# Experts ranked by their tokens on the chip: four of eight work on 64 slots instead of 96

## What is computed

```python
def swiglu(h, w1, w3, w2):
    return (jax.nn.silu(h @ w1) * (h @ w3)) @ w2

def moe_swiglu(h, w_r, b_r, w1, w3, w2):
    logits = (hf @ w_r).astype(jnp.float32) + b_r.astype(jnp.float32)
    top_v, top_i = lax.top_k(logits, TOP_K)          # 2 of 8
    gates = jax.nn.softmax(top_v, axis=-1)
    combine = jnp.sum(jax.nn.one_hot(top_i, N_EXPERTS) * gates[..., None], axis=-2)
    for e in range(N_EXPERTS):
        out = out + combine[:, e:e + 1] * swiglu(hf, w1[e], w3[e], w2[e])
```

## Time and profile before

| | |
|---|---|
| median of three runs | 1546.9 us (1544.61 to 1548.57) |
| the profiled execution | 1545.36 us, of which the span from the first to the last instruction is 1543.2 us |
| PE busy | 1482.5 us, 96% of the span |
| weight loads of PE | 856.9 us, 56% |
| DVE / ACT busy | 544.0 us (35%) / 409.7 us (27%) |
| moved by DMA | 396.39 MB, of which 388.84 MB by the queue of SP |

### The profile page before, as it was taken

The page is one execution under the profiler, slowest core; times in us unless marked ns, Lnnn a source line. Parts: engine busy times, 40 slices in busy tenths (PEclk is TensorE's granted clock), DMA queues, the critical chain, the costliest instruction groups (busy, mean ns, idle before and its releaser), DMA issues.

```text
span 1543.2 us, 27247 instructions
## 1 busy us (share of the span) xinstructions
PE 1482.5 (96%) x12261; PEld 856.9 (56%) x12261; DVE 544.0 (35%) x967; ACT 409.7 (27%) x719; POOL 4.1 (0%) x8
## 2 busy tenths in 40 slices
PE   6899889999999999898889999999999999999997
PEld 3688558888888888787673333333333333333332
DVE  2899884432323333779741110020111002011112
ACT  3522684422222222665830011010001101000001
POOL 0000000000000000000000000000000000000010
PEclk9999899999999999999989999999999999999999
DMA  9988702623321433313167999999999999999991
GB/s 352 385 302 321 281 29 82 208 67 109 109 82 39 152 105 114 110 55 148 44 246 261 396 407 342 408 355 411 403 402 407 343 408 366 410 398 382 408 382 43
DMA packets 147323, 396.39 MB, mean 257 GB/s; under 512 B 7584, under 2 KB 38848, under 8 KB 147200
## 3 DMA queue, kind: packets, MB, share of 16 engines
q1 hardware_dynamic: 144000, 388.84, 66.8%
q10 hardware_dynamic: 2624, 3.63, 0.7%
q0 software_dynamic: 576, 2.10, 0.4%
HBM read 390.74 MB, written 3.80 MB: 256 GB/s over the span
## 4 chain that ended last, share of the span: by engine, by line
PE 88%; DVE 6%; DMA 3%; ACT 1%; SPq 1%; issue 1%; DVEq 0%; ACTq 0%
PE bank L1107 30%; PE bank L1137 10%; PE bank L953 5%; PE bank L954 5%; PE bank L952 5%; PE bank L1145 5%; PE bank L675 4%; PE bank L676 3%; PE bank L677 3%; DMA weight_ring<-in_w_ada 3%; PE bank L961 3%; PE bank L962 2%; PE bank L963 2%; PE bank L621 2%; DVE weight_ring L1793 1%; DVE slot_halves L1700 1%
## 5 line engine op out<-in xcount | busy, mean ns | idle before, releaser
L1107 PE MATMUL bank<-weight_ring,gathered 128*32 128x512 f32 (+1 forms) x4608 | 464.1, 557 | 0.0
L1107 PEld LDWEIGHTS bank<-weight_ring,gathered 128*32 128x32 f32 x4608 | 146.5, 110 | 291.9 <-issue 290.7
L1137 PE MATMUL bank<-weight_ring,scratch 128*32 128x512 f32 x1360 | 165.9, 592 | 0.0
L2138 DVE TENSOR_TENSOR scratch<-scratch,bank 64x512 f32<-64x512 f32 (+1 forms) x72 | 46.0, 639 | 316.9 <-ACT scratch L1608 314.0
L954 PE MATMUL bank<-slot_halves,slot_halves 128*128 128x512 f32 x336 | 130.7, 389 | 0.0
L953 PE MATMUL bank<-hT_halves,slot_halves 128*128 128x512 f32 x336 | 130.7, 389 | 0.0
L952 PE MATMUL bank<-slot_halves 128*128 128x512 f32 x320 | 124.6, 389 | 0.0
L1793 DVE SCALAR_TENSOR_TENSOR weight_ring<-scratch,conv_weights,weight_ring 128x512 f32<-128x512 f32 (+1 forms) x207 | 121.3, 636 | 2.6 <-ACT weight_ring L1385 0.7
L676 PE MATMUL bank<-hT_halves,slot_halves 128*128 128x512 f32 (+1 forms) x352 | 121.6, 346 | 0.0
L675 PE MATMUL bank<-slot_halves,slot_halves 128*128 128x512 f32 (+1 forms) x284 | 105.4, 371 | 8.1 <-DVE slot_halves L1700 5.2
L1608 ACT ACTIVATE scratch<-bank 64x512 f32<-64x512 f32 (+1 forms) x72 | 40.1, 557 | 230.1 <-PE bank L1107 229.2
(11 more groups left out here) (298 smaller groups left out, 1681.1 us busy)
## 6 DMA issues: line engine op xcount, KB each, us to landing
weight_ring<-in_exp_w SPq DMA_DIRECT2D x216, 1024.0 KB, 10.0
weight_ring<-in_w_ada SPq DMA_DIRECT2D x24, 2048.0 KB, 13.6
weight_ring<-in_exp_w SPq DMA_DIRECT2D x64, 768.0 KB, 8.1
weight_ring<-in_ffn_w SPq DMA_DIRECT2D x33, 1024.0 KB, 5.4
weight_ring<-in_w_in SPq DMA_DIRECT2D x8, 1024.0 KB, 15.4
weight_ring<-in_w_out SPq DMA_DIRECT2D x4, 2048.0 KB, 11.4
weight_ring<-in_w_in SPq DMA_DIRECT2D x2, 3072.0 KB, 15.2
expert_rows<-scratch ACTq DMA_DIRECT2D x14, 128.0 KB, 6.0
```

Of the source, the lines that this page charges most:

```text
L1107: i = mm(ps[BLOCK * job:BLOCK * (job + 1), 0:cw], gathered_block(e, k, b), w[:, kk, a * cw:(a + 1) * cw], start=(k == 0), stop=(k == KT - 1))
L1137: i = mm(bank[6][quarter, :], at01[:, c0:c0 + BLOCK], w2[:, i_, half * 512:(half + 1) * 512], start=(first and i_ == 0), stop=(last and i_ ...
```

## The change

- Position 0 stays expert 0. On the positions 1 to 7 stand the experts 1 to 7 in an order that DVE works out in `ranked`: by their number of tokens, the four with the fewest on the positions 1, 3, 5 and 7 (`SMALL`), the three with the most on 2, 4 and 6.
- The positions in `SMALL` have two blocks (64 slots), the others three. For the small ones `pair` and `gated` do two blocks, L1090, L1145 and the copy for block 2 fall away, and so do the rows of block 2 in `rows_shifted`, `rows_scaled`, `rows_kept_of` and `scatter` (position 7 is a small one).
- Three rounds are run if any position holds more tokens than its slots.
- SP reads the expert of each position from 1 to 7 from a table in SBUF (`value_load`, after a wait on `most_ready`) and forms the address of each weight load from that register.
- The gathers are one expert ahead of the stage (96 columns instead of 192), three from g = 1 on and four from g = 7 on; `select(1)` stands ahead of the groups. PE waits ahead of `residual_rows` for the counts and no longer for `most_ready`.
- `rows_found` works with slots and first rows by position; 32 columns are added to the constants.

```diff
+SMALL = [1, 3, 5, 7]
+LARGE = [i for i in range(NE) if i not in SMALL]
+RANK_OF_POSITION = [0] + [1 + (SMALL + LARGE[1:]).index(i) for i in range(1, NE)]
+BLOCKS_OF = [2 if i in SMALL else BLOCKS for i in range(NE)]
+BLOCK_ORDER = [[1, 0] if i in SMALL else [0, 1, 2] for i in range(NE)]
 SELECTS = 4
-PLACE = [3, 4, 5, 6, 7, 1, 2, 0]
-GATHERS = [(0, 1), (2, 3, 4), (7, 5, 6)]
+PLACE = [3, 4, 5, 6, 1, 2, 3, 0]
+GATHERS = [(0,), (1, 2, 3), (7, 4, 5, 6)]
...
             def expert_weights(r):
+                expert = {}
+
+                def of_expert(name, e):
+                    return t[name][0, e] if e == 0 else t[name][0, bass.ds(expert[e], 1)].rearrange("a k n -> (a k) n")
+
                 def first(g):
                     e, j = divmod(g, CH)
                     w = WIDTH[j]
+                    if e and j == 0:
+                        sp.wait_ge(most_ready, 1)
+                        expert[e] = sp.value_load(expert_at[0:1, e:e + 1], min_val=0, max_val=NE - 1)
                     for p in range(KT // 2):
                         for m, name in enumerate(["exp_w3", "exp_w1"]):
                             v = UNITS * r + H_UNIT[g, p, m]
-                            load(v, unit(v, w), t[name][0, e].rearrange("(k p) n -> p k n", p=P)[
+                            load(v, unit(v, w), of_expert(name, e).rearrange("(k p) n -> p k n", p=P)[
                                 :, 2 * p:2 * p + 2, j * 1024:j * 1024 + w])
...
-                            i = mm(ps[:, c * 2 * C:(c + 1) * 2 * C], rows_, sel_first[n],
+                            i = mm(ps[:, c * C:(c + 1) * C], rows_, sel_first[n],
...
             def scatter(n):
 
-                for v, rows_ in ((0, rows_01), (1, rows_2)):
-                    for half in range(2):
-                        part = slice(HD * half, HD * half + HD)
-                        i = mm(bank[SCATTER_BANK[2 * n + half]][:, :], to_token[part, n, v, :], rows_[part, :],
-                               start=(v == 0), stop=(v == 1))
-                        if v == 1:
-                            i.then_inc(scatter_mm, 1)
+                for half in range(2):
+                    part = slice(HD * half, HD * half + HD)
+                    mm(bank[SCATTER_BANK[2 * n + half]][:, :], to_token[part, n, :], rows_01[part, :],
+                       start=True, stop=True).then_inc(scatter_mm, 1)
 
             def experts(r):
...
-                    pe.wait_ge(a_tok, 3 * (NG * r + g) + 3)
-                    for q in range(nq):
-                        i = pe.transpose(s2[:, q * HD:(q + 1) * HD], act_2[:, q * P:(q + 1) * P], ident[0:HD, 0:HD])
-                    i.then_inc(a_mm, 1)
+                    if g // CH not in SMALL:
+                        pe.wait_ge(a_tok, before_group(g, r, 2, 3) + 3)
+                        for q in range(nq):
+                            i = pe.transpose(s2[:, q * HD:(q + 1) * HD], act_2[:, q * P:(q + 1) * P], ident[0:HD, 0:HD])
...
                     for kk in range(2):
                         k = 2 * p + kk
-                        for b in range(BLOCKS):
+                        for b in BLOCK_ORDER[e]:
                             ps = sums(g, b)
+                            last = b == BLOCK_ORDER[e][-1]
                             for job in range(4):
                                 w = w1 if (job < 2) == (b == 1) else w3
                                 a = job % 2
                                 i = mm(ps[BLOCK * job:BLOCK * (job + 1), 0:cw], gathered_block(e, k, b),
                                        w[:, kk, a * cw:(a + 1) * cw], start=(k == 0), stop=(k == KT - 1))
-                                if kk == 1 and b == BLOCKS - 1 and a == 1:
+                                if kk == 1 and last and a == 1:
                                     i.then_inc(unit_done, 1)
-                            if k == KT - 1 and b < BLOCKS - 1:
+                            if k == KT - 1 and not last:
...
-                        if i_ == 0:
+                        if i_ == 0 and e not in SMALL:
...
-                            pe.wait_ge(most_ready, 1)
+                            pe.wait_ge(pos_ready, 2)
...
+            def ranked():
+
+                dve.wait_ge(pos_ready, 2)
+                square = parts[:, 0:NE * NE].rearrange("p (i e) -> p i e", e=NE)
+                link(stt(out=key, in0=held_by, scalar=float(NE), in1=con[:, KEY:KEY + NE], op0=ALU.mult, op1=ALU.add))
+                link(tt(square, across(key, NE), down(key), ALU.is_lt))
+                link(dve.reduce_sum(rank, square, AX))
+                link(tt(of_position, across(rank, NE), down(con[:, RANK:RANK + NE]), ALU.is_equal))
+                for n in range(2):
+                    link(tt(square, of_position, across(pv[:, :, n], NE), ALU.mult))
+                    link(dve.reduce_sum(placed[:, :, n], square, AX))
+                link(by_position(at_position, con[:, IOTA:IOTA + NE]))
+                dve.tensor_copy(expert_at[:, :], at_position)
+                link(by_position(over, held_by))
+                link(tt(over, over, con[:, CAP:CAP + NE], ALU.subtract))
+                link(dve.reduce_max(den[:, 0:1], over, AX))
+                ts(most[:, :], den[:, 0:1], float(C), None, ALU.add).then_inc(most_ready, 1)
...
-                if e == NE - 1:
-                    tt(rows_2, bank[7][:, :], gate_b, ALU.mult).then_inc(yt_ready, 1)
-                else:
+                if e not in SMALL:
                     for half in range(2):
...
+                    counted()
                     gates()
-                    fullest()
+                    ranked()
                     rows_copied()
+                select(1)
+                if r == 0:
+                    places_of_experts()
                 for g in range(NG):
                     e, j = divmod(g, CH)
                     if e and j == 1:
                         rows_scaled(e - 1, r)
-                    if g:
+                    if g and (g - 1) // CH not in SMALL:
                         second_turned(g - 1)
```

More of the change, by code:

```diff
@@ L91, with slots, first_row, before @@
 H_UNIT, Y_UNIT, UNITS = unit_numbers()
+def slots(i):
+    return BLOCK * BLOCKS_OF[i]
+def first_row(i):
+    return sum(slots(p) for p in range(i))
+def before(i, r, small, large):
+    each = [small if p in SMALL else large for p in range(NE)]
+    return r * sum(each) + sum(each[:i])
+def before_group(g, r, small, large):
+    return before(g // CH, r, CH * small, CH * large) + (g % CH) * (small if g // CH in SMALL else large)
 CONSTS = ["ident", "mean_d", "mean_head", "mean_conv", "rot", "halves", "before", "ones"]
@@ L98 @@
 REV = IOTA + ROUNDS * C
-NCONST = REV + NE
+KEY = REV + NE
+RANK = KEY + NE
+CAP = RANK + NE
+LINE = CAP + NE
+NCONST = LINE + NE
 def backbone(nc, t, out):
@@ L472, in fills_at, with fill_sums, kept_before @@
             e, j = divmod(g, CH)
[L473 to L476, removed]
+            return [(e // 2 + 1, 4 * (j - 1) + spot)] if e in (0, 2) and j else []
+        def fill_sums(g, spot):
+            return sums(g - 1, 2 - spot % 2)
         FIRST_FILL_BANK = [7, 6, 5, 3]
         SCATTER_BANK = [0, 1, 2, 5]
+        def kept_before(i, r):
+            each = [32 if p in SMALL else 64 for p in range(NE - 1)]
+            return r * sum(each) + sum(each[:i])
         pv = posm[:, 0:2 * NE].rearrange("p (e n) -> p e n", n=2)
         cv = comb[:, 0:2 * NE].rearrange("p (e n) -> p e n", n=2)
+        placed, gate_last = (att[:, a:a + n].rearrange("p (e n) -> p e n", n=2) for a, n in ((16, 2 * NE), (32, 2)))
+        of_position = scr[:, 7424:7488].rearrange("p (i e) -> p i e", e=NE)
+        parts = scr[:, 7488:7616]
+        key, rank, held_by, at_position, over, slots_by, line_by = (att[:, 40 + i * NE:48 + i * NE] for i in range(7))
         def rounds(eng, body, end):
@@ L541, in second @@
                         f0 = j * 1024 + u * 256
-                        load(v, unit(v, D), t["exp_w2"][0, e][f0:f0 + 256, :].rearrange("(q p) n -> p q n", p=P))
+                        load(v, unit(v, D), of_expert("exp_w2", e)[f0:f0 + 256, :].rearrange("(q p) n -> p q n", p=P))
                 for g in range(NG):
@@ L1149, in experts @@
                 if r:
[L1150 removed]
+                    pe.wait_ge(yt_ready, before(0, r, 1, 2))
                     pe.wait_ge(scatter_added, 4 * r)
@@ L1574, in rows_kept_of @@
             def rows_kept_of(e, r):
-                done = 2 * (NE * r + e)
                 if r:
                     act.wait_ge(row_back, 64 * r)
-                for z, (rows_, b, n) in enumerate([(rows_01, 0, HD), (rows_2, 2, BLOCK)]):
-                    act.wait_ge(yt_ready, done + z + 1)
+                for z, (rows_, b, n) in enumerate([(rows_01, 0, HD), (rows_2, 2, BLOCK)][:BLOCKS_OF[e] - 1]):
+                    act.wait_ge(yt_ready, before(e, r, 1, 2) + z + 1)
                     for half in range(2):
```

(23 more changed lines are left out.)

164 lines of the change are left out of this document (91 added, 73 removed).

## The result

The changed kernel takes 1504.5 us (median of four runs, 1504.3 to 1506.0), the kernel before 1547.4 us in the same session: ratio 0.9728, 95% interval 0.9711 to 0.9744. It is faster by 2.7%, and 18 us slower than the 1486 us forecast. The profiled execution's span is 1504.1 us, against the 1486.0 us of the sum.

What follows compares the result with a forecast made beforehand. PE set the pace with DMA close behind; after the change DMA would bound: stream from 858.5 us, plus 613.2, 2.7 and 11.6 us, a span of 1486.0 us. Forecast 1486 us, range 1468 to 1506 us.

Steps and rivals of the forecast that it cites:

- The mechanism: Expert stage: the bound moves from PE to DMA, the ring runs empty and bytes set the end, 613 us.
- A: Expert stage: PE stays the bound and its whole saving counts, 1424 us; chance 0.02.
- C: SP's weight loads: a register address makes each issue longer than 2.7 us, about 1560 us at 3 us; chance 0.03.
- D: Small positions: an expert there exceeds 64 tokens, so three rounds run, about 2850 us; chance 0.02.
- E: Expert stage: 391 GB/s is DMA's own mean, so almost nothing changes, 1544 us; chance 0.04.
- B: Small positions: PE's waits lower its clock, up to 1652 us if all run at 1.2 GHz; chance 0.04.
- Landing times: Weight loads in the expert stage: time from issue to landing grows to 30 us and more.
- PE's busy time: Whole kernel: PE's busy time falls by about 118 us.
- The head: Start of the stage: `gather_first` gains 1.5 us (bounds 0 to 3.4); later gathers lie where PE waits anyway.
- The rate: Saturated stretch: DMA moves 251.4 MB at 410 GB/s; a rate of 415 to 400 means -7 to +15 us.
- The end of the stream: Last weight loads: the stream ends at 1471.7 us; only a low clock was allowed for, 0 to +5 us.
- The tail: After the stream: 2.7 us for semaphore and last product, then 11.6 us (13.3 less 1.7) to the span's end.

Runs made afterwards that it cites:

- all_small: The changed kernel with all seven positions 1 to 7 at two blocks and the overflow check off: 1504.2 us, ratio 0.973.
- half_bytes: The changed kernel with each weight load of the four small positions bringing only half of its unit, PE's work unchanged: 1431.6 us, ratio 0.926.
- const_addr: The changed kernel with the expert addresses of positions 1 to 7 written as constants in place of the register: 1505.4 us, ratio 0.9739.
- in_flight_5: The changed kernel with SP issuing a weight load only once the load five places back has landed: 1505.0 us, ratio 0.9733.
- thin_fills: The changed kernel with the eight gathers in position 0 doing one matmul of four: 1503.6 us, ratio 0.9729.
- rows_later: The changed kernel with residual rows and gate rows moved from position 0 into position 1, same result: 1502.6 us, ratio 0.9714.

## Why the prediction was right, and where it was off

**The mechanism was right.** DMA's bytes set the end (all_small, half_bytes), PE's own time would have been some 1430 us, and the ring runs empty. PE's idle time by DMA is 41.9 us ahead of the pairs and 12.2 ahead of the products with w2, near the 60 us named; nearly all of it lies in positions 3, 5 and 7, the first 1.9 us between 980 and 1000 us in position 2. SP's waits for PE fall from 478.6 to 106.2 us between 900 and 1478 us. Of the rivals, A is the time without the bytes; C is refuted by const_addr; D did not come, one round was run; E is refuted by 407 GB/s over 578 us. The clock of B did fall, to 0.91 and 0.83 in single windows of 20 us, but over 900 to 1478 us it was 0.99, though the waits ahead of the pairs (27 of them, 1.6 us in the mean, 4.3 at the longest) were longer than the 0.8 to 1.7 us that the prediction counted on; and all_small, with 0.95 there and more waiting, is no slower.

**Two signs did not come.** Landing times were to grow to 30 us and more; they are 18.1 us in the median and 24.2 at the most, because SP stands in its issue once about seven loads are under way and doesn't queue the whole ring. And PE's busy time was to fall by 118 us; it fell by 98. In half_bytes, with the same work and no waits, it falls by 113.5, so 15 us of the gap are the slower matmuls of a PE that waits (567 ns for 559 in the pairs). With DMA as the bound neither cost anything.

**A sum of a rival was wrong.** In C, 3 us an issue would be 0.28 us too much in each of 248 units on top of an unchanged 1547 us: about 1616 us and not 1560.

**The sum was 18.1 us short**, in four terms. The median, 1504.5 us, is inside the range by 1.5 us, and there was some luck in that: the head and the end of the stream left the bounds that the prediction gave them (+1.5 and +5 us), and the rate used only 4 of its 15.

*The head: 7.4 us.* The prediction took 1.5 us of gain from `gather_first` and put the gathers for positions 1 to 3 where "PE waits anyway". In 800 to 900 us DMA moved 28.2 MB, against 30.6 MB before, where 0.6 MB more was expected: 3.0 MB at 407 GB/s are 7.4 us. (These two profiles can be compared so: their stages start within 0.06 us of each other.) One part is `gather_first` itself (now L1086). Its chain at the start of the stage in in_flight_5, which has the same code there, beside the earlier trace rows:

```profile
801.41 7.03 PE bank L1088 x32
808.44 11.87 PE bank L1162 x96
```

Half the columns take 7.03 us for 32 matmuls, no less than before (6.71): from start to start 0.21 us with 96 columns as with 192, at a granted clock of 0.50. So the lower bound of the estimate (nothing saved) was the right end. And the 96 records behind it take 11.87 us in place of 10.44: in the kernel before the clock is at 1.00 from 808 us on, in the changed kernel from 812. Why it rises later is not shown. The changed kernel itself has 7.03 and 11.85 us and is done with these records 1.8 us later than the kernel before; with the 1.5 us of gain that did not come, that is 3.3 of the 7.4 us. The other part, 4.1 us, are eight gathers (L1097) that lie in position 0 now, from 840.6 us on, ahead of saturation, when the first later gather of the kernel before starts at 897.58 us. They take PE eight times 0.72 us, 5.8 us, and there each us of PE delays the freeing of places. Here PE did not "wait anyway". thin_fills and rows_later agree: from the stage's start the last load lands 2.3 to 2.6 us sooner than in the changed kernel's two profiles for 3.1 us of PE's work, and 3.1 to 3.4 sooner for 3.4; both lie outside the scatter of the four kernels with the changed head (685.1 to 686.9), by 0.8 and 1.6 us.

*The rate: 4.2 us.* 407 GB/s were measured for the 410 taken, over 578 us. It is within the range of 405 to 415 and just under the 408 to 413 named as a sign.

*The end of the stream: 5.3 us.* In its last 11 us DMA moves 212 GB/s, 2.3 MB that at 407 take 5.7 us. The prediction let the stream stop at full rate, as it does in the kernel before. Its last windows at full rate and behind it, and then two of the changed kernel:

```profile
1500.00:1502.00 2.00, 2.00 (x31) 0.80 (x27) 2.00 (x3) 0.00 (x0) 0.00 (x0) 1.00 1.01 403
1502.00:1504.00 2.00, 2.00 (x32) 0.84 (x28) 2.00 (x2) 0.00 (x0) 0.00 (x0) 1.00 0.45 174
...
1480.00:1482.00 2.00, 1.91 (x16) 0.41 (x16) 0.00 (x0) 1.09 (x1) 0.00 (x0) 1.00 0.69 260
1484.00:1486.00 2.00, 1.06 (x16) 0.25 (x12) 0.00 (x0) 0.00 (x0) 0.00 (x0) 1.00 0.49 201
```

It is not the low clock for which the prediction gave this end up to 5 us: the clock is 1.00 there. The cause stays open: five loads under way don't cure it, and nothing read from the trace here tells the 16 engines apart.

*The tail: 1.1 us net.* 15.4 us from the last landing to the end, for 1.0 + 1.7 + 11.6 = 14.3 worked out. The semaphore and the last product took 2.0 us and not 2.7. Behind them the scatter is 1.0 us shorter and DVE's 0.69 us are gone, as worked out, but 1.80 us of idle time for the branch came in their place: 13.4 for 11.6. In the kernel before there are 0.2 us between DVE and the scatter; that PE's sequencer ran ahead of the array there and hid the branch is the explanation that fits, and no run shows it directly.

So the steps that failed are the sizes of the head (a gain of 1.5 us was expected, and the later gathers were put at nothing) and of the end of the stream, which had no term; the four together are 7.4 + 4.2 + 5.3 + 1.1 = 18.0 us.

## What to carry to other kernels

When two resources stand close together, a cut of one is worth the distance to the other and no more: here 118 us of PE's work gave 43 us. What decides then is how early the second one is saturated and how it ends: work of the old bound ahead of saturation costs about one for one (so rows_later has it, within its scatter), the same work behind it is free (all_small), so it is moved there. An engine that now waits at the end of the kernel shows costs that were covered before, such as the read and the branch on a count. And a gain of 1 to 4 us is read from the start of the changed stage on, since what lies ahead of it moved by up to 3.7 us between profiles.

## What was not expected of the hardware

- SP's issue of a 1 MB load takes 2.2 us in the median once about seven loads are under way (18.1 us to landing), and 0.37 us below that, with a constant as with a register address.
- Five loads under way keep 406 GB/s, three only 393 GB/s.
- A read of a count, the branch on it and the instructions behind it keep PE idle for 4.5 to 4.8 us; which of the three, the runs don't tell.
- In the low-clock start of the stage a matmul of 128 rows with 96 columns takes as long from start to start (0.21 us) as one with 192.
- PE stood 27 times for weights ahead of the pairs, up to 4.3 us, and was busy for 524.7 of 578 us; the granted clock was 0.99 over that stretch.
